# Where key norms, exponentials and constants stand in the scan of an RWKV block

## The reference, cut to what matters

```python
w_logit = w0 + tanh(xw @ w1) @ w2                 # per direction
decay = exp(-exp(-softplus(-w_logit) - 0.5))
a = sigmoid(a0 + (xa @ a1) @ a2)                  # per direction
kk = split_heads(k * k_k)
kk = kk / maximum(norm(kk, axis=-1), 1e-12)       # the key norms
k_dir = k * (1.0 + (a - 1.0) * k_a)
def step(s, inp):                                 # scan over tokens, both directions
    rt, wt, kt, vt, at, bt = inp                  # at = -kk, bt = kk * a
    sa = einsum('bhij,bhj->bhi', s, at)
    s = s * wt + sa[..., None] * bt[:, :, None, :] + vt[..., None] * kt[:, :, None, :]
    return s, einsum('bhij,bhj->bhi', s, rt)
y = (y_f + y_b - mean) * rsqrt(var + 64e-5) * lnx_w + lnx_b + sum(r * k_dir * r_k) * v
```

## Time and profile before

| | us |
|---|---|
| median of 3 runs | 3717.08 |
| the runs | 3716.05, 3722.02, 3717.08 |
| profiled execution, own time | 3724.84 |
| profiled execution, span | 3723.0 |
| PE busy in the span | 3426.0 (92%) |
| DVE busy | 1632.2 (44%) |
| ACT busy | 1179.5 (32%) |
| POOL busy | 394.4 (11%) |

### The profile page before, as it was taken

The page is one execution under the profiler, slowest core; times in us unless marked ns, Lnnn a source line. Parts: engine busy times, 40 slices in busy tenths (PEclk is TensorE's granted clock), DMA queues, the critical chain, the costliest instruction groups (busy, mean ns, idle before and its releaser), DMA issues.

```text
span 3723.0 us, 79537 instructions
## 1 busy us (share of the span) xinstructions
PE 3426.0 (92%) x35550; PEld 2659.8 (71%) x35550; DVE 1632.2 (44%) x3121; ACT 1179.5 (32%) x2462; POOL 394.4 (11%) x616
## 2 busy tenths in 40 slices
PE   7898998999999799799999997999999899799998
PEld 5767877788888388688888895588878677433332
DVE  3354455433333732466666663443443474312112
ACT  3342233312212332355555543222233332200001
POOL 0000122000000100232222221000010300000000
PEclk8999999999999899899999997899999899799999
DMA  4493162211111110000000002122211122689996
GB/s 177 149 352 111 51 241 108 79 58 68 68 61 54 65 46 23 10 5 5 5 5 4 5 5 99 46 91 102 102 66 46 47 104 76 264 353 412 414 428 293
DMA packets 35237, 437.42 MB, mean 117 GB/s; under 512 B 5024, under 2 KB 5632, under 8 KB 9168
## 3 DMA queue, kind: packets, MB, share of 16 engines
q1 hardware_dynamic: 29664, 413.44, 27.8%
q0 software_dynamic: 5232, 18.89, 1.6%
HBM read 425.49 MB, written 6.82 MB: 116 GB/s over the span
## 4 chain that ended last, share of the span: by engine, by line
PE 80%; DMA 7%; DVE 6%; ACT 5%; issue 1%; POOL 0%; SPq 0%; DVEq 0%; ACTq 0%; POOLq 0%
PE ps L750 23%; PE ps L2045 8%; PE ps L2047 8%; PE ps L2046 8%; PE ps L2461 7%; PE ps L3816 6%; DMA part<-in_wu 4%; PE ps L2454 3%; PE ps L1005 2%; PE ps L2468 2%; PE ps L2576 1%; ACT L71 1%; PE ps L2567 1%; DMA part<-in_wd 1%; PE ps L1322 1%
## 5 line engine op out<-in xcount | busy, mean ns | idle before, releaser
L750 PE MATMUL ps<-part 128*128 128x256 f32 (+1 forms) x4848 | 879.3, 343 | 40.9 <-DVE part L990 15.5
L750 PEld LDWEIGHTS ps<-part 128*128 128x128 f32 x4848 | 756.5, 193 | 160.6 <-issue 19.1
L2045 PE MATMUL ps<-part 128*128 128x512 f32 (+1 forms) x1536 | 549.6, 358 | 18.0 <-DVE part L2092 11.4
L2046 PE MATMUL ps<-part 128*128 128x512 f32 (+1 forms) x1536 | 548.8, 357 | 0.0
L2047 PE MATMUL ps<-part 128*128 128x512 f32 (+1 forms) x1536 | 548.6, 357 | 0.0
L3816 PE MATMUL ps<-part 128*64 128x512 f32 x1536 | 374.8, 606 | 27.4 <-DMA part<-in_wg 12.2
L2069 DVE TENSOR_TENSOR part<-part 128x1024 fp32r<-128x1024 f32 x128 | 158.3, 1237 | 497.7 <-ACT part L2058 497.7
L2461 PE MATMUL ps<-part 64*64 64x64 f32 x9984 | 344.7, 220 | 20.5 <-ACT part L2784 11.9
L2461 PEld LDWEIGHTS ps<-part 64*64 64x64 f32 x9984 | 319.1, 136 | 51.2 <-ACT part L2784 12.9
L2045 PEld LDWEIGHTS ps<-part 128*128 128x128 f32 x1536 | 289.7, 189 | 68.5 <-DVE part L2092 12.6
L2046 PEld LDWEIGHTS ps<-part 128*128 128x128 f32 x1536 | 290.5, 189 | 46.9
(11 more groups left out here) (418 smaller groups left out, 4362.9 us busy)
## 6 DMA issues: line engine op xcount, KB each, us to landing
part<-in_ada_w SPq DMA_DIRECT2D x36, 2048.0 KB, 9.7
part<-in_mlp_w SPq DMA_DIRECT2D x32, 2048.0 KB, 7.5
part<-in_wg SPq DMA_DIRECT2D x32, 2048.0 KB, 14.1
part<-in_wu SPq DMA_DIRECT2D x32, 2048.0 KB, 13.0
part<-in_wd SPq DMA_DIRECT2D x32, 2048.0 KB, 14.3
part<-in_b_in SPq DMA_DIRECT2D x8, 2048.0 KB, 7.7
part<-in_ab_w_in SPq DMA_DIRECT2D x7, 2048.0 KB, 8.3
part<-in_rkv SPq DMA_DIRECT2D x6, 2048.0 KB, 7.5
```

The lines of the kernel that those rows point to most:

```text
L750: mm = pe.e.matmul(ps[:, j * n:j * n + n], lhs, rhs, start=k == ks[0] and i == 0, stop=k == ks[-1] and i == 2)
L2045: pe.e.matmul(ps, wh[:, k, :], hi[:, k, x0:x1], start=k == 0, stop=False)
L2046: pe.e.matmul(ps, wh[:, k, :], lo[:, k, x0:x1], start=False, stop=False)
```

## The change

Four edits, all in the scan.

1. The exponentials L2803, L2805, L2811, L2813 take whichever of the tables 0 and 6 is in (`exp()`).
2. The key norms' last two steps move: logarithm and exponential from turn 4 to turn 6, product and copy of the turned rows from turn 5 to turn 7, and the turning on PE from turn 4 to turn 7. Turn 6 is also the turn of the end's logarithm.
3. The first group's key norms ran in a unit's time of their own (n = -2) ahead of the first preparation; now both run in n = -1.
4. POOL issues the four loads of weights before the nine of constants, and DVE waits for the constants only before the first mask of the solve, not before the scan's first instruction.

```diff
+    def exp(self):
+
+        if self.held not in (0, 6):
+            self.table(0)
...
+KEYS = {0: 0, 1: 1, 2: 2, 3: 3, 6: 4, 7: 5}
 PREP = {1: 0, 3: 1, 4: 2, 5: 3, 6: 4, 7: 5, 8: 6, 9: 7}
 END = {TURNS: 0, TURNS + 2: 1, TURNS + 4: 2, TURNS + 6: 3, TURNS + 8: 4, TURNS + 10: 5}
...
-    for n in range(-2, UNITS + 2):
+    for n in range(-1, UNITS + 2):
+        keys = 0 if n < 0 else (n + 2) // 3
         for turn in range(TURNS):
-            if (n + 2) % 3 == 0 and (n + 2) // 3 < 8 and turn <= 5:
-                yield "kk", turn, (n + 2) // 3
+            if (n < 0 or n % 3 == 1) and keys < 8 and turn in KEYS:
+                yield "kk", KEYS[turn], keys
...
-        if what == "kk" and turn == 4:
+        if what == "kk" and turn == 5:
             for j, (x0, x1) in enumerate(BOTH):
                 ps = K.bank("v turned", u, j)
...
-    v.wait_ge(*[K.at("rw const", n) for n in sorted(cn)], K.at("rw", "vec"), K.at("rw", "wa0"))
+    v.wait_ge(K.at("rw", "vec"), K.at("rw", "wa0"))
...
+            if turn == 0 and not u.n:
+                v.wait_ge(*[K.at("rw const", n) for n in sorted(cn)])
...
             if turn == 3:
                 s.wait_ge(K.at("B mid", *u.key))
-                s.exp_tanh()
+                s.exp()
...
             if turn == 5:
-                s.exp_tanh()
+                s.exp()
...
+    for d in range(2):
+        weights(d, 0)
     for n in sorted(K.rw.cn):
         K.load(pool, K.rw.cn[n], K.const_src(n), "rw const", n)
-    for d in range(2):
-        weights(d, 0)
```

## The result

| | before | changed kernel |
|---|---|---|
| median, us | 3717.84 (4 runs) | 3682.70 (4 runs) |
| lowest and highest | 3716.05, 3722.02 | 3678.45, 3687.18 |
| profiled execution, own time | 3724.84 | 3678.45 |
| scan, last copy before it to its last instruction | 793.6 | 759.4 |

A forecast was written before the change was run, and what follows sets the result against it. PE bounds the kernel, ACT only where PE waits for it. Terms -11.9 - 17.2 - 9.8 + 6.7 + 1.3 - 7.1 - 1.3 = -39.3 us from the 3717.08 median give 3678 us; 8-in-10 range 3668 to 3693.

The forecast's parts named there:

- The reading: Whole scan: PE is 80% of the chain, ACT 5%, so ACT counts only where PE stands and waits for it.
- Part 1: Logarithm and turned rows leave turns 4 and 5: PE's 7 waits on the turned rows go, -11.9 us.
- Part 2: Turns 6 and 7: PE's waits before L2567 go, except 1.3 us left in n = 22, -17.2 us.
- The clock term: Behind the waits before L2567: seven clock dips of 1.4 us, read as following the long wait, go, -9.8 us.
- Part 3: New table load ahead of the tanh: 0.95 us of wait in seven units, +6.7 us, and +1.3 in n = 0.
- The drain of 1380 ns with each switch: Rival: each new load in turn 1 also drains ACT, new waits 11 us longer, 3689 us; chance 0.04.
- Part 4: Start of the scan: the first product of the solve comes 7.1 us earlier, -7.1 us; bounds 4 and 9.3.
- Part 5: Tail: the last end no longer loads table 6, -1.3 us.

The follow-up runs named there:

- the maximum in turn 2: Changed kernel with DVE's maximum of the key norms in turn 2 instead of turn 3: ratio to before 0.9880, scan 752.5 us.

## Why the prediction was right, and where it was not

The kernel was forecast at 3678 us and came to 3682.7; the gain at 39.3 and came to 35.1 by the medians, 34.2 in the scan. Point by point:

- *The reading* that only ACT in front of PE counts held. Edit 1 alone took off the two loads before L2567 and nothing else, and its 19 us (22 in the scan) came from there.
- *Part 1*, -11.9 us: the waits went in full, but were worth less. The period shrank by 1.3 us (edit 1 alone against edits 1 and 2) where 1.77 was waited. The step that fell short is "What is late next is the solve itself, which in units without key norms leaves PE no such wait". PE now comes to the turned inverse too soon: L2475 starts at 1741.98, released by DVE L2706, 0.81 us behind the start of L2574 (1741.17), where 0.47 us lay between the two before (1759.48 and 1759.95). The wait on the turned rows had covered these 0.3 us. The turning in its new place adds only 0.05 (1.62 us for 1.57).
- *Part 2*, -17.2 us: right. "PE and ACT arrive together; I take no wait" held with 0.6 us to spare for ACT: one more load, in the run without edit 1, made a wait of 0.68.
- *The clock term*, -9.8 us: the size was right and the reason wrong. From before to edit 1 alone the period shrank by 3.3 us. The wait of 2.65 went, and the tanh wait, worth 1.0, came: so the dip was worth 3.3 - 2.65 + 1.0 = 1.6 us, against 1.4 forecast. But "I read it as a consequence of the long wait", with 1.78 us taken as a length that draws none, is refuted by the dip behind 1.49, the missing one behind 2.85, and the missing ones behind the old 2.65 in n = 13 and n = 19 with edit 4 alone. I took seven dips out of seven for a rule, where they were seven repeats of one and the same pattern. What the Trainium skill says there, and I set aside, was the better guide. It was partly luck that no dip remained in the units.
- *Part 3*, +6.7 and +1.3: right, the seven at 1.0 each. In n = 0 the wait was 1.35 against 0.18 before, 1.2 of the 1.3 forecast, but the stretch to n = 1 cost 2.9 us in all. Its projections ran at half clock there: 1.23 and 1.07 us against 0.76 and 0.60 before, 0.9 us more; the rest is in small delays behind, 0.3 of it in a wait of 0.57 us that was 0.24 before. The forecast had no term for the low clock of the start reaching further into unit 0. It missed by 1.6 us in this trace, and by 0.4 to 1.6 in the three others with the same unit 0 (29.6, 29.9 and 30.7 us). The drain of 1380 ns with each switch that the Trainium skill gives ("ScalarE: Activation LUTs", section "What ACT_TABLE_LOAD costs") did not appear: load at 1762.44, tanh at 1763.73.
- *Part 4*, -7.1: 7.0, and its steps too: the running sum 9.2 us nearer (9.3 said), 10.4 us from it to the first product (10.5 said). The last tenths are luck: the other executions with this start give 6.4 to 6.6. And the credit belongs to edit 4 alone, which the prediction could have seen: its own chain put the norms behind the projections, and the running sum behind the norms.
- *Part 5*, -1.3: the load went, yet the last stretch fell 2 us short of its forecast. PE's first product of the last end (L2591) took 1.96 us at a clock of 0.5, and 1.12 before: 0.8 of the 2. The two behind it ran at the low clock before as well. The same code took 1.12 us with edits 1 and 2 alone and with the maximum in turn 2. Why the clock falls earlier in one execution than in another stays open. Some 0.4 us more is part 1's shortfall in n = 19; the rest was not followed up.

By the table of landmarks the scan missed by 5.1 us: 2.0 in the last stretch, 1.6 in unit 0, 1.1 in the five steady periods (part 1 short by 0.4 each, the dips better by 0.2), 0.4 up to n = 4. Against that, part 2 came in full, part 1 to about 3 us, and the dips in full though for a wrong reason.

## What to carry to other kernels

Take the worth of an instruction from the slack at the place where it stands: the same 1.28 us load was worth 2.65 with its twin ahead of a copy for PE, 0.8 to 1.0 ahead of the tanh, and nothing in turn 8, where ACT idles. Two edits that clear the same wait do not add up (19 us alone, none beside the other); try each alone before both are kept. A wait taken away is worth less than its length when another engine's result comes due within it (1.3 of 1.77 here). And a pattern that repeats with the loop is one observation, however often it stands in the trace.

## What the runs showed of the hardware

- A granted clock near 0.5 for about 3 us can follow a wait of PE of 1.49 us and can fail to follow one of 2.85 us; of 29 waits of 2.6 to 2.7 us 26 had one. It cost 1.6 us where it fell, 0.9 to 1.6 by the next group's norms.
- Of several table loads in a row without a function between them only one was left in the program that ran (6 of 21 added, and waits of PE of 0.68 us whatever the number).
- The same three products ahead of the scan's end took 1.96, 2.08 and 1.88 us in one execution and 1.12, 1.12 and 1.02 in another, at a granted clock of about 0.5 and of 1.00.
- The same code ahead of the scan took up to 9 us more or less from one kernel's profiled execution to another's (last copy at 1501.3 to 1510.4), a quarter of the whole effect: compare stages by landmarks within them.
